# Halves' rows of 544 columns at other addresses, and the second layer's context keys by a scan

## The reference

```python
def gla_final_state(k, v, logf):
    g = jnp.cumsum(logf, axis=2)
    return jnp.einsum('bhsk,bhsv->bhkv', k * jnp.exp(g[:, :, -1:, :] - g), v)
...
        if last:
            s_f = gla_final_state(kfc, vhc, lffc)
            s_b = gla_final_state(_flip_t(kbc), _flip_t(vhc), _flip_t(lfbc))
```

## Time and profile before

| | us |
|---|---|
| median of 3 runs | 1942.03 (1940.7 to 1943.5) |
| profiled execution | 1941.69 |
| its span | 1939.7 |
| TensorE busy | 1889.4 (97%) |
| VectorE busy | 1229.7 (63%) |
| ScalarE busy | 944.8 (49%) |
| GpSimd busy | 475.1 (24%) |
| chain that ended last: TensorE's share | 78% |
| the same, VectorE's share | 11% |

### The profile page before, as it was taken

How to read it: one execution, slowest core, us unless ns; L and a number is a source line. 1 busy time by engine, 2 the same in 40 slices (tenths; PEclk the granted TensorE clock), 3 DMA queues, 4 the chain that set the end, 5 groups by cost and what they waited for, 6 DMA issues and landing times.

```text
span 1939.7 us, 31204 instructions
## 1 busy us (share of the span) xinstructions
PE 1889.4 (97%) x12606; PEld 1668.0 (86%) x12606; DVE 1229.7 (63%) x1975; ACT 944.8 (49%) x1508; POOL 475.1 (24%) x328
## 2 busy tenths in 40 slices
PE   8999999999999999999999999999999899999999
PEld 8989988999988887777788888888898898799988
DVE  6888898779856943666663743354376947776410
ACT  6444446655456443426733531233265554765643
POOL 2211022000000000003344354555500000304887
PEclk9999999999999999999999999999999999999999
DMA  8987663567733112221123354466632343154554
GB/s 300 272 255 260 198 226 129 178 226 237 272 119 100 64 55 87 87 66 44 66 98 130 109 163 141 153 216 210 178 102 98 117 132 123 65 174 146 182 194 152
DMA packets 83951, 297.12 MB, mean 153 GB/s; under 512 B 9704, under 2 KB 12912, under 8 KB 83552
## 3 DMA queue, kind: packets, MB, share of 16 engines
q1 hardware_dynamic: 65600, 232.81, 36.4%
q0 software_dynamic: 16592, 58.79, 10.0%
q10 hardware_dynamic: 1616, 3.52, 0.5%
HBM read 294.02 MB, written 2.54 MB: 153 GB/s over the span
## 4 chain that ended last, share of the span: by engine, by line
PE 78%; DVE 11%; ACT 4%; issue 3%; DMA 2%; POOL 1%; DVEq 0%; SPq 0%; ACTq 0%; POOLq 0%
PE ps L598 20%; PE ps L593 20%; PE ps L596 20%; DVE wl L461 4%; PE ps L590 3%; DMA wr<-wstream 2%; ACT wh L445 2%; PE ps L592 1%; PE ps L1277 1%; PE ps L1381 1%; PE ps L1282 1%; PE ps L1279 1%; PE ps L1421 1%; PE ps L2162 1%; PE ps L1400 1%
## 5 line engine op out<-in xcount | busy, mean ns | idle before, releaser
L593 PE MATMUL ps<-HH,wh 128*128 128x256 f32 (+1 forms) x2160 | 703.4, 326 | 1.3 <-DVE K L2428 0.9
L598 PE MATMUL ps<-HH,wl 128*128 128x256 f32 (+1 forms) x2160 | 691.6, 320 | 12.1 <-DVE wl L461 9.9
L596 PE MATMUL ps<-HL,wh 128*128 128x256 f32 (+1 forms) x2160 | 690.0, 319 | 0.0
L445 ACT ACTIVATE wh<-wr 128x1024 fp32r<-128x1024 f32 x440 | 459.2, 1052 | 331.0 <-PE ps L598 231.0
L461 DVE TENSOR_TENSOR wl<-wr,wh 128x1024 fp32r<-128x1024 f32 x301 | 366.4, 1221 | 188.2 <-ACT wh L445 187.4
L598 PEld LDWEIGHTS ps<-HH,wl 128*128 128x128 f32 x2160 | 406.9, 188 | 47.1 <-DVE wl L461 13.7
L593 PEld LDWEIGHTS ps<-HH,wh 128*128 128x128 f32 x2160 | 407.2, 189 | 41.7 <-issue 6.6
L596 PEld LDWEIGHTS ps<-HL,wh 128*128 128x128 f32 x2160 | 407.3, 189 | 33.3 <-issue 2.4
L461 POOL TENSOR_TENSOR wl<-wr,wh 128x1024 fp32r<-128x1024 f32 x139 | 337.3, 2429 | 211.9 <-ACT wh L445 205.3
L1536 POOL TENSOR_TENSOR s<-s,ST 128x512 f32<-128x512 f32 x56 | 57.3, 1040 | 665.2 <-DVE ST L1504 665.0
L1134 DVE CUSTOM_DVE_ANT_0 PROD<-WM,COND 128x1024 f32<-128x1024 f32 x104 | 129.8, 1261 | 1.3
(11 more groups left out here) (312 smaller groups left out, 2967.6 us busy)
## 6 DMA issues: line engine op xcount, KB each, us to landing
wr<-wstream SPq DMA_DIRECT2D x440, 512.0 KB, 3.4
WM<-wmod POOLq DMA_DIRECT2D x68, 512.0 KB, 4.5
X<-wmod POOLq DMA_DIRECT2D x28, 512.0 KB, 6.6
NAB<-naskew POOLq DMA_DIRECT2D x16, 128.0 KB, 7.5
DILB<-dilskew POOLq DMA_DIRECT2D x8, 256.0 KB, 8.2
COND<-cond ACTq DMA_DIRECT2D x2, 1024.0 KB, 4.6
X<-xin SPq DMA_DIRECT2D x4, 256.0 KB, 5.5
HL<-cond ACTq DMA_DIRECT2D x1, 1024.0 KB, 7.8
```

What stands on the lines that cost most here:

```text
L445: ins = e.activation(self.WH[i % NSPL][:, :], self.WR[n % NRAW][:, :], ACT.Copy)
L593: e.matmul(out, wh, xh, start=i == 0, stop=False)
L596: e.matmul(out, wh, xl, start=False, stop=False)
L598: return e.matmul(out, wl, xh, start=False, stop=i == n_k - 1)
```

## The change

LINE, to which the halves and the arena are aligned, goes from 64 to 128 bytes, and so the row of the halves from 528 to 544 columns and the wide views' start from 16 to 32 columns in. All short views start 8 columns (32 bytes) in. In layer 1, K and F are raised and joined over 256 columns only, level 7's raising of K is left out there, and the sum of the keys is over 256 columns. The context's keys are instead made by VectorE in the forget stage: for each direction and head a scan over the context's forget factors (running backwards in direction 0) leaves the products in a new buffer DK, and one product multiplies K by them. Direction 0's stand between the heads of direction 1, direction 1's after its last head. The transposes wait for these.

```diff
-LINE, PAST = 64, 32
+LINE, PAST = 128, 32
 ROW = 512 + LINE // 4
...
         self.wide_halves = [x[:, :, LINE // 4:ROW] for x in halves]
-        self.short_halves = [[x[:, :, n:n + 256] for x in halves] for n in (4, 2)]
+        self.short_halves = [x[:, :, PAST // 4:PAST // 4 + 256] for x in halves]
...
+        self.DK = at_("DK", 80.5, [2, 4, 256])
...
-        return self.short_halves[l is not None] if l is None or l and i else self.wide_halves
+        return self.short_halves if l is None or l and i else self.wide_halves
...
                 w.wait_ge(*v.at((l, "f", 1, h)))
-                ins = e.tensor_tensor(r, self.K[0][:, h, :], k, ALU.add)
+                T = 256 if l else 512
+                ins = e.tensor_tensor(r[:, 0:T], self.K[0][:, h, 0:T], k[:, 0:T], ALU.add)
...
                 total(h)
                 if h:
                     ratio(h - 1)
+                if l:
+                    self.dve_context_k(e, w, l, 0, h)
             ratio(3)
+            if l:
+                for h in range(4):
+                    self.dve_context_k(e, w, l, 1, h)
+
+    def dve_context_k(self, e, w, l, dr, h):
+        v, p = self.c("fg_v"), self.DK[:, dr, h, 0:255]
+        ones = self.ones[:, 0:1]
+        ones = bass.AP(ones.tensor, ones.offset, [list(ones.ap[0]), [0, 255]])
+        f, k = self.F[dr][:, h, 256:512], self.K[dr][:, h, 256:512]
+        if dr:
+            f, out, k = f[:, 0:255], p, k[:, 1:256]
+        else:
+            f, out = (bass.AP(x.tensor, x[:, 254:255].offset, [list(x.ap[0]), [-1, 255]]) for x in (f[:, 1:256], p))
+            k = k[:, 0:255]
+        for x in self.a_free(l):
+            w.wait_ge(*x)
+        w.wait_ge(*v.at((l, "f", dr, h)))
+        e.tensor_tensor_scan(out, f, ones, 1.0, ALU.mult, ALU.mult).then_inc(*v.mark((l, "decay", dr, h)))
+        w.wait_ge(*v.at((l, "decay", dr, h)))
+        e.tensor_tensor(k, k, p, ALU.mult).then_inc(*v.mark((l, "context", dr, h)))
...
         for z in range(2):
-            self.dve_raise_k(e, w, l, 7, z)
+            if l == 0:
+                self.dve_raise_k(e, w, l, 7, z)
             self.dve_raise_q(e, w, l, 7, z)
...
-        ins = self.dve_raise(e, self.K[z], z, 1 << lv, z, 256 if lv == 7 else 0, 512)
+        ins = self.dve_raise(e, self.K[z], z, 1 << lv, z, 256 if lv == 7 else 0, 256 if l else 512)
...
+        if lv == 7:
+            w.wait_ge(*self.c("r_t").at((l, 6, z)))
...
     def dve_join(self, e, w, l, lv, z):
-        f = self.F[z][:, :, :].rearrange("p h t -> p (h t)")
-        f0, f1 = (self.side(f, 1 << lv, u)[:, :, 0] for u in range(2))
+        if l:
+            f0, f1 = (self.head_side(self.F[z][:, :, 0:256], 1 << lv, u)[:, :, :, 0] for u in range(2))
+        else:
+            f = self.F[z][:, :, :].rearrange("p h t -> p (h t)")
+            f0, f1 = (self.side(f, 1 << lv, u)[:, :, 0] for u in range(2))
...
-                w.wait_ge(*self.c("r_ku").at((l, 8, z)))
+                w.wait_ge(*(self.c("fg_v").at((l, "context", z, 3)) if l else self.c("r_ku").at((l, 8, z))))
```

## The result

| | before | after |
|---|---|---|
| median of 20 runs each, us | 1941.45 | 1943.45 |
| lowest and highest, us | 1938.64, 1943.73 | 1941.57, 1948.08 |
| ratio after/before | | 1.0015, 95% interval 1.0009 to 1.0022 |
| span of the profiled execution, us | 1939.7 | 1942.5 |

By the medians the changed kernel is slower by 2.0 us (0.10%), by the ratio of all runs by 0.15%, 2.9 us. Either counts as no change by the bound of 0.2%. The forecast was 1933.4, ten microseconds less, and the range (1921 to 1943) ended half a microsecond too low. The interval leaves out 1.000, so the sign is real, if small.

What follows compares the result with a forecast made beforehand. TensorE, busy in 97% of the span, was taken as the bound, VectorE in layer 1's recurrence. Terms 4.8 - 4.9 + 4.1 + 2.4 - 1.3 + 0 + 3.5 = 8.6 us gave 1933.4, range 1921 to 1943.

Steps and rivals of the forecast that it cites:

- the first term: HH and HL, 2184 matmuls of 512 columns: alternating rows bring 231.9 ns to about 229.5, 4.8 us gained.
- HIDH, HIDL, YA, YB: 888 matmuls on arena operands moving from 128 past to 0 past 256: 226.7 to 232.2 ns, 4.9 us lost.
- Short rows: HH's 256-column views, first block and layer 1's ff1 and branches: toward 116.6 ns, 4.1 and 2.4 us gained, bounds 0 and 8.8.
- NHH: NHH and NHL, 1056 matmuls moving from 160 to 32 past: no change, bounds 3.5 us either way.
- Wide rows 256 wide: HH's wide rows used 256 wide, 1104 matmuls: from 118.3 toward 119.8 ns, 1.3 us lost, bounds 0 and 1.7.
- The scans: VectorE's part in layer 1: recurrence gains 5.5 us, delayed wl stops TensorE 2.0; net 3.5 us gained (0.5 to 6).
- unequal is always dear: Rival: alternating rows never get cheap, HIDH and Y lose 4.9, NHH goes to 119.9; 1948.6 us, chance 0.12.
- Both its points: Where that rival decides: NHH's pitch passes 118.5 and HH's 512-column pitch stays above 231.
- Multiple of 128 is enough: Rival: any multiple of 128 bytes gives the cheap 512-column pitch, HIDH losing nothing; 22.0 us gained, 1920, chance 0.13.
- the address has no part: Rival: HH differs by something other than address, only VectorE's 3.5 us is left; 1938.5, chance 0.05.
- the scan is dear: Rival: a scan takes 1.5 us, TensorE stands 5.5, the recurrence's gain is eaten; 1937 (1941 at 2.5 us), chance 0.08.
- the slower rival: The rival "unequal is always dear": 1948.6 us, chance 0.12, left out of the range to 1943.

Runs made afterwards that it cites:

- rows of 576: Changed kernel with rows of 576 columns (2304 bytes), arena at 128 past a multiple of 256, ST and RT in spare bytes: 1926.54 us, ratio to before 0.9927.
- layout alone: Kernel before with only the new layout (rows of 544 columns, short rows 32 bytes in, arena rounded to 128), old recurrence: 1946.68 us, ratio 1.0039.
- scans alone: Changed kernel with the layout of before (rows of 528 columns, old offsets), keeping the scan and all that goes with it: 1936.87 us, ratio to before 0.9977.
- 16 past: Rows-of-576 kernel with NHH, NHL and HID1 16 bytes into the arena instead of 32: 1927.07 us, ratio to before 0.9928.
- rows of 576 with the scans moved: Rows-of-576 kernel with direction 1's context products moved between the weight halves of the row products: 1920.11 us, ratio to before 0.9903.

## Why the prediction was wrong, point by point

- **The step that failed is the first term**, HH and HL at 512 columns: 4.8 us gained by the forecast, 1.1 lost, 5.9 of the ten microseconds. The reading behind it was right (equal modulo 256 is what is cheap, in the earlier trace rows), but I took the odd rows at the cheap pitch after "some matmuls" and did not hold that number against the three matmuls that each k has in the dense products. After the change, layer 0's products with HH stationary show it; the rows are the first, seventh and last matmul of k = 3 (equal) and the first of k = 4 (unequal) and of k = 5:

```profile
623.29 0.40 PE L1278 MATMUL ps<-wh,HH 128*128 128x512 f32 x1
...
624.68 0.39 PE L1278 MATMUL ps<-wh,HH 128*128 128x512 f32 x1
...
625.81 0.40 PE L1283 MATMUL ps<-wh,HL 128*128 128x512 f32 x1
626.05 0.40 PE L1278 MATMUL ps<-wh,HH 128*128 128x512 f32 x1
...
628.84 0.40 PE L1278 MATMUL ps<-wh,HH 128*128 128x512 f32 x1
```

  The first six steps take 1.39 us, 231.7 ns each; the next five 1.13 us, 226 to 228 each within the rounding; k = 4 takes 2.79 us for twelve, 232.5. In k = 5 and 7 it is the same. In k = 1, also equal, three steps take 0.70 us (233 each) and the eight behind them 1.81 us, 226 to 227 each. So an equal row pays the dear pitch for its first three to seven matmuls, and in groups of three it never gets out of it. The earlier trace rows already said so: there k = 7 reached 226.7 from its seventh matmul and from its fourth on. The rows of 576 settled it.
- **HIDH, HIDL, YA, YB**: 4.9 us lost by the forecast, 5.0 measured. This reading from addresses alone, for operands that the diff does not name, is the part that held best.
- **Short rows**: 6.5 us gained by the forecast, 4.3 measured, inside its bounds. I had 116.6 for three quarters of them; all settled at 117.8. In the profile, 1.5 of layer 1's 2.1 went to the clock in ff1, which no part of the prediction had. The layout alone took 116.7 in ff1 at the same addresses, so that the address does not fix this pitch.
- **NHH** at no change (bounds 3.5 either way): 1.4 lost. **Wide rows 256 wide**: 1.3 lost by the forecast, 0.7 measured. Y1 went down, 120.0 to 118.7, though it stays on a multiple of 128. OHH and OHL, 512 columns in the arena, were left out of the sum: 0.4 lost.
- **The scans**: 3.5 us net by the forecast; 3.5 by the run of the scans alone (2.7 to 6.2 by its interval), 2.9 by the stages of the changed kernel's trace. That it came out is in part luck, because inside it two errors cancel. The recurrence gave 6.9 and not 5.5: I had left TensorE 1.5 us of idle time, and one pause of 0.8 is left. The stop is 2.4 and not 2.0, because the scan takes 0.68 and not 0.6, and the 1.6 us of slow clock behind it was not forecast.
- **The rivals**: "unequal is always dear" had the mechanism (alternating rows never reach the cheap pitch) and most of its prices, but put the short rows at nothing and NHH at 119.9, so its 1948.6 is five too high. Both its points were met (NHH at 118.7 in the first feed-forward, HH above 231). I held it at 0.12 because NHH, unequal, had 116.6, and that argument mixed two things: what an unequal place costs at 256 columns says nothing of whether alternating rows are cheap at 512. "Multiple of 128 is enough" fell with HIDH at 232.4, "the address has no part" with the same number, "the scan is dear" with the scan's 0.68 us.
- **The range** left out what it should have held by 0.45 us. Its upper end was taken just inside the slower rival; the case "HH gains nothing and the rest as forecast" gives 1933.4 + 4.8 = 1938.2 and was in it, but with NHH's bound of 3.5 and half of the short rows' gain gone (3.2) it reaches 1944.9. Mis-sized terms of one sign were what the upper end had no room for.

## What to carry to other kernels

Find, from the allocation order, where moving and stationary operands lie to each other modulo 256 bytes, and make the row pitch a multiple of 256 so that all rows share the good place: rows of 2304 bytes in place of 2176 made 9.6 us of difference, with the arena's place the same. A cheap steady state counts only if its entry is shorter than the run of equal instructions: read how many steps the entry takes, then count how many the loop gives. And when work is put on an engine ahead of an operand that the bounding engine awaits, look first for that engine's own waits further on; moved behind the first wl, the same scans cost nothing.

## What the runs showed of the hardware

- 512 columns have two pitches in this kernel, 226.7 and 232 ns, by the operands' places modulo 256 relative to each other; three to seven matmuls lie between them. Why the place matters no run here shows. The Trainium skill, "TensorE: Matmul & The Clock Gate", section "Wait — 56ns, not 53.3ns?", would give 215.7 ns for both; no stretch here at the full clock comes under 226.
- 256 columns have at least six levels: 113.4, 116.7, 117.3, 117.8, 118.7 and 120.0. NHH shows two of them at the same addresses within one execution (118.7 and 113.4 with 16 past), and HH in ff1 of layer 1 two between kernels (117.8 in the changed one, 116.7 in the layout alone). What came before seems to choose; that is argued and not shown.
- TensorE's granted clock fell to the 1.2 GHz level at a stop of 2.3 to 2.6 us in the row products of each of the six kernels that have it, between the stop's last 0.2 us and 1.6 us behind its end (0.427 us per 512-column matmul at that level). In layer 1's ff1 it fell in the profiles of eight of the ten kernels, the layout alone among them, and stayed up in those of before and of rows of 576 with the scans moved. The length of the pause does not decide: two matmuls in 2.82 us ended in a fall with the scans alone and in none before, and two in 3.14 us in a fall with rows of 576 and in none with the scans moved as well. What does is open. A stop can thus cost more than its length: 2.4 us came to 4.0.
- A scan of 255 elements takes 0.68 us on VectorE, the product of the same length 0.42.
